# A four-layer hybrid backbone: one activation on ScalarE and two steps on VectorE take another place in the order

## The chip, the cores and the metric

The kernel runs on one core of a Trainium2 chip. The core has five engines that run their own instruction streams and meet at semaphores: TensorE (PE, matrix products), VectorE (DVE), ScalarE (ACT), GpSimd (POOL) and SyncE (SP), which here only issues loads. The time of a run is the device time of one execution in microseconds. Of the kernel before there are three runs.

## The reference

Four layers run over 256 context tokens and 256 latent tokens of width 1024, with the mixers A, B, C, A. A is a bidirectional Mamba-2 (SSD) mixer, B grouped-query attention, C a pooling mixer. Each layer is modulated by a vector (shift, scale, gate) from a matrix product with `mod_w`, and ends in a layer norm:

```python
for i in range(DEPTH):
    shift_x, scale_x, gate_x = split(sc @ mod_w[i] + mod_b[i], 3)
    hx = x * (1 + scale_x) + shift_x                  # the same for hc from ctx
    out_x, out_c = mixer(hx, hc, ...)                 # A, B, C, A
    x = layer_norm(ALPHA * x + gate_x * out_x)        # and ctx, but for the last layer
```

The pooling mixer (layer 2) splits its projection into `u` and `z`. `u` falls into four groups of 512 channels, each with a window of 2, 4, 8 or 16 tokens:

```python
pooled = centred_mean(u_g, window) - u_g
out = ((pooled @ group_w[g]) * layer_scale * silu(z_g)) @ w_out
```

The SSD mixer (layers 0 and 3) projects to x, B, C and a gate z, passes x, B and C through a depthwise convolution of 5 taps and a SiLU, and scans forwards and backwards in chunks of 128 tokens. Within a chunk the scores C B^T are masked (lower triangle forwards, upper backwards), weighted by head and by decay, and applied to x. In the last layer only the latent tokens' output is wanted, so only the two latent chunks are scored.

## The kernel before

All products with weights are made from fp32 values split in two: ACT copies a loaded unit to a rounded high half (`act_split`, L377), DVE subtracts it for the low half (`dve_split`, L384), and PE makes three passes (`three_pass`, L415 to L417). A unit is 128 x 1024 values, 512 KB. SP loads the units in the order of the list `items` into `raw`, a ring of four slots. A slot is loaded again once the unit in it is used up: for a weight, once its low half is written (`lo_done`), for a piece of `mod_w`, once PE has summed it (`mod_summed`). The weights themselves sit in a ring of four pairs.

The order of the work is written out by hand, for each engine on its own; there is no scheduler. Each engine runs its stream in order.

Layer 3 (SSD) goes over eight groups in a pipeline: step i projects group i and scans group i - 1. PE projects tiles 0 to 3 (two of x, one of B, one of C) and two of z into PSUM banks. On ACT, `ssd_act_step` makes the middle tap of tile k (`first_tap(k)`, L735), and on DVE `ssd_dve_step` adds the other four (`taps(k)`, L901). DVE's `masks()` (L919) makes the forward and the backward masked scores `cb` of the scanned group; `cb_dt(n)` on ACT (L766) weights the backward ones of chunk n, four heads each, and `weigh_steps` on DVE (L928) adds the forward part that POOL made. The order on DVE in a step is `taps(0)`, `masks()`, `gate` (L980), `taps(1)`, then the two splits of z, `weigh_steps`, and so on. Layer 0 has the same functions; it runs `first_tap(1)` behind `cb_dt`, where layer 3 runs it in front.

Layer 2 (pooling) goes over four groups g. PE projects four tiles of u, then four of z, and after each of the first three z tiles it sums one piece of the next layer's modulation (`pe_mod_sum`, L444), and turns the one before it (`pe_mod_turn`, L469) after ACT has copied its rows (L464). Then it applies the group weights. For each u tile t, ACT copies it to `up`; DVE makes the window sums (`lev`, L2348, one instruction for a window of 2 up to four for 16), scales (L2358) and subtracts (L2360) into `pf`; ACT rounds `pf` to `p_hi` (L2329) and DVE subtracts for `p_lo` (L2366). In between, DVE splits the four units of z: two, called (g, 0), after tile 1's sums, two, called (g, 1), in front of tile 3's. The list `items` has for each group: four units of u, four of z, six of modulation (three pieces of two halves), two of group weights. So the six modulation units follow the z units through the ring: the first piece takes the slots of z (g, 0), the second those of z (g, 1), the third those of the first. DVE also adds the bias to each turned piece (`dve_mod_col`, L476) and in groups 0 and 1 scales and shifts the residual (`dve_resid`, L1549 and L1553, four instructions over 1024 columns).

Of the kernel before, what the change touches and what calls it, by code (L numbers as in the profile page):

```python
# [3 lines left out]
def backbone(nc, ins, out, depth=4):  # L4
# [153 lines left out]
    def last_layer(L):  # L158
        return L == DEEP - 1
# [44 lines left out]
    for L in range(depth):  # L204
        more = L + 1 < depth
# [173 lines left out]
    def dve_split(dve, *key, width=UNIT):  # L379
        r = R_OF[key]  # L380
        hi, lo = w_place(key)
        dve.wait_ge(raw_full[r % RS], LOADS[r])
        dve.wait_ge(hi_done, W_OF[key] + 1)
        dve.tensor_tensor(lo[:, 0:width], raw[:, r % RS, 0:width], hi[:, 0:width].bitcast(F32),  # L384
                          ALU.subtract).then_inc(lo_done, 1)
# [20 lines left out]
    def dve_split2(dve, *key):  # L406
        for a in range(2):
            dve_split(dve, *key, a)
# [22 lines left out]
    def mod_at(L, q):  # L431
        return MOD_PIECES * L + q
# [40 lines left out]
    def dve_mod_col(dve, L, q, b, col=0):  # L473
        dve.wait_ge(mod_turned, mod_at(L, q) + 1)
        bias = par[:, 0, 24 * L + 2 * q:24 * L + 2 * q + 2].unsqueeze(2).broadcast_to((128, 2, 2))
        dve.tensor_tensor(mod_col[:, L % 2, 2 * q:2 * q + 2, :],  # L476
                          bank[b][:, col:col + 4].rearrange("p (t s) -> p t s", s=2), bias,
                          ALU.add).then_inc(mod_done, 1)
# [7 lines left out]
    def p_poolscale():  # L486
        return par[:, 1, 64:80]
# [17 lines left out]
    def scan_done(L, g, name):  # L505
        jobs = scan_jobs(L)
        return len(jobs) * g + jobs.index(name) + 1
# [7 lines left out]
    def proj_bank(i, k):  # L515
        return bank[proj_index(i, k) % 4]
# [15 lines left out]
    def c_of(g):  # L532
        return xcc[:, :] if g % 2 else xc[:, 3, :]
# [182 lines left out]
    def ssd_act_step(act, L, i):  # L716
        s = lay[L]
        g = i - 1
# [5 lines left out]
        def first_tap(k):  # L724
            if k == 3:
                if i >= 2:
                    act.wait_ge(s["scan_p"], scan_done(L, i - 2, "it3"))
                dst, a = c_of(i), t0
            else:
                if g >= 0:  # L730
                    act.wait_ge(s["t1_p"], 4 * g + (4 if k == 2 else k + 1))
                dst, a = xc[:, k, :], 0
            what = "x" if k < 2 else "bc"
            act.wait_ge(s[what + "_p"], 3 * i + 1 + 2 * (k % 2))
            act.activation(dst[:, a:], proj_bank(i, k)[:, a:], ACT.Identity, scale=gp[:, i, 6 * k + 2:6 * k + 3],  # L735
                           bias=gp[:, i, 6 * k + 5:6 * k + 6]).then_inc(s["tap_a"], 1)
# [23 lines left out]
        def cb_dt(n):  # L760
            c = first + n
            act.wait_ge(s["cbm_d"], 2 * g + 2)
            if nc * g + n >= 2:
                act.wait_ge(s["m_d"], nc * g + n - 1)
            for h in range(HG):
                last = act.activation(Wb[:, n % 2, h, :], cb[:, 1, c, :], ACT.Copy,  # L766
                                      scale=sg[:, g, 48 + 4 * c + h:49 + 4 * c + h])
            last.then_inc(s["cbdt_a"], 1)
# [63 lines left out]
        if has_ssd:  # L832
            turned()
        first_tap(0)
        if last_layer(L):
            first_tap(1)
        if has_ssd:
            cb_dt(0)
            cb_dt(1)
        if not last_layer(L):  # L840
            first_tap(1)
        if i == 0:
            first_tap(2)
            ssd_act_cum(act, L)
# [551 lines left out]
    def dve_ylo(dve, L, c):  # L1396
        s = lay[L]
        t0 = SEG if last_layer(L) else 0
        dve.wait_ge(s["yhi_a"], c + 1)
        hi = yhi_of(L, c)[:, t0:].bitcast(F32)  # L1400
        if L % 3 == 0:
            dve.wait_ge(s["sq_a"], c + 1)
            dve.scalar_tensor_tensor(ylo[:, c, t0:], ys[:, c, t0:], p_normg(L // 3)[:, c:c + 1], hi,
                                     ALU.mult, ALU.subtract).then_inc(s["ylo_d"], 1)
        else:
            dve.tensor_tensor(ylo[:, c, t0:], ys[:, c, t0:], hi, ALU.subtract).then_inc(s["ylo_d"], 1)
# [136 lines left out]
    def dve_resid(dve, L, tiles):  # L1543
        s = lay[L]
        dve.wait_ge(s["ln_loaded"], s["base"]["ln_loaded"] + 32)
        for n, tt in enumerate(out_tiles(L + 1)):
            if tt in tiles:
                dve.wait_ge(s["turn_p"], s["base"]["turn_p"] + 2 * tt + 2)
                dve.tensor_tensor(resid[:, tt, :], resid[:, tt, :], lng_b[:, :], ALU.mult).then_inc(s["resid_d"], 1)  # L1549
        dve.wait_ge(s["resid_d"], s["base"]["resid_d"] + resid_count(L, tiles, 1))  # L1550
        for n, tt in enumerate(out_tiles(L + 1)):
            if tt in tiles:
                dve.tensor_tensor(resid[:, tt, :], resid[:, tt, :], lnb_b[:, :], ALU.add).then_inc(s["resid_d"], 1)  # L1553
# [666 lines left out]
    def pool_steps(w):  # L2220
        return [m for m in (2, 4, 8, 16) if m <= w]
# [4 lines left out]
    def pool_tile_end(n):  # L2226
        g, t = divmod(n, 4)
        return pool_ops_before(g) + (t + 1) * (len(pool_steps(WINDOWS[g])) + 2)
# [102 lines left out]
    def pool_dve(dve, L):  # L2331
        s = lay[L]
        more = L + 1 < depth
        T = Tally(s["pool_d"])
        for g in range(4):
            w = WINDOWS[g]
            for t in range(4):
                n = 4 * g + t
                dve.wait_ge(s["up_a"], n + 1)
                if t == 3:  # L2340
                    dve_split2(dve, L, "z", (g, 1))
                src = up[:, t % 2, :, :]
                for lv, m in enumerate(pool_steps(w)):
                    a, b = PADL - w // 2, PADL - w // 2 + SEG + w - m
                    dst = lev[:, lv % 2, :, :]
                    if T.n:
                        T.wait(dve)
                    T.inc(dve.tensor_tensor(dst[:, :, a:b], src[:, :, a:b], src[:, :, a + m // 2:b + m // 2], ALU.add))  # L2348
                    src = dst
                T.wait(dve)  # L2350
                if n:
                    dve.wait_ge(s["plo_d"], n)
                    dve.wait_ge(s["phi_a"], n)
                else:
                    dve.wait_ge(s["tab_loaded"], 16)
                a = PADL - w // 2
                inv = invc[:, g, :].unsqueeze(1).broadcast_to((128, 2, SEG))
                T.inc(dve.tensor_tensor(two(pf[:, :]), src[:, :, a:a + SEG], inv, ALU.mult))  # L2358
                T.wait(dve)
                T.inc(dve.tensor_tensor(two(pf[:, :]), two(pf[:, :]), up[:, t % 2, :, PADL:PADL + SEG], ALU.subtract))  # L2360
                assert T.n == pool_tile_end(n)
                if t == 1:
                    dve_split2(dve, L, "z", (g, 0))
                dve.wait_ge(s["phi_a"], n + 1)
                T.wait(dve)
                dve.tensor_tensor(p_lo[:, t, :], pf[:, :], p_hi[:, t, :].bitcast(F32), ALU.subtract).then_inc(s["plo_d"], 1)  # L2366
            if more:
                dve_mod_col(dve, L + 1, 3 * g, 6)
            if g < 2:
                dve_resid(dve, L - 1, (2 * g, 2 * g + 1))  # L2370
            if more:
                dve_mod_col(dve, L + 1, 3 * g + 1, 7)
            dve_split2(dve, L, "gw", g)
            if more:
                dve_mod_col(dve, L + 1, 3 * g + 2, 6)
            if g == 3:
                for c in range(4):
                    dve_ylo(dve, L, c)
            for t in range(4):
                n = 4 * g + t  # L2380
                dve.wait_ge(s["mix_p"], 5 * g + t + 1 + t // 3)
                dve.wait_ge(s["zs_a"], 4 * g + 4)
                dve.scalar_tensor_tensor(ys[:, n, :], bank[6 + t % 2], p_poolscale()[:, n:n + 1], zs[:, t, :],
                                         ALU.mult, ALU.mult).then_inc(s["mix_d"], 1)
                if g < 3 and t == 1:
                    dve_split2(dve, L, "u", (g + 1, 0))
                if g == 3 and t == 1:
                    for c in range(2):
                        dve_split(dve, L, "out", c, 0)
            if g < 3:  # L2390
                dve_split2(dve, L, "u", (g + 1, 1))
        for c in (2, 3):
            dve_split(dve, L, "out", c, 0)
        for c in range(4, 12):
            dve_ylo(dve, L, c)
        for c in range(4, 12):
            dve_split(dve, L, "out", c, 0)
        dve_out(dve, L, 12)
# [237 lines left out]
```

## Time and profile before

| | |
|---|---|
| median of 3 runs | 1572.9 us (1571.96 to 1574.02) |
| the profiled execution | 1572.9 us, span 1571.7 us |
| PE busy | 1469.3 us (93% of the span) |
| DVE busy | 1129.2 us (72%) |
| ACT busy | 712.8 us (45%) |
| POOL busy | 328.8 us (21%) |
| granted TensorE clock, mean | 0.970 |
| layer 2, group 1 of the pooling, of 60.00 us | PE busy 59.59, DVE 32.99, ACT 17.68 us |

The busy shares are means over four layers with different limits, and overlapping matmuls count as busy. What a place is worth is seen from its own stretch. In a timeline row the columns are the start in us from the span's start, the length in us, the engine, the line in the kernel, the operation, out<-in with the tiles' names (`ps` is PSUM) and shapes, and xN where N instructions were merged; in brackets is the idle time before it and what ended it. Rows of one engine may overlap a little, since an instruction begins before the one in front has quite ended.

### The profile page before, as it was taken

The numbers are of one execution on the slowest core, as the hardware profiler recorded it, in microseconds if no ns is written. First come the engines' busy times: TensorE is split into PE (matmuls) and PEld (weight loads), VectorE is DVE, ScalarE is ACT, GpSimd is POOL, SyncE is SP. The second block draws the span as 40 slices with busy tenths as digits, with TensorE's granted clock in tenths as the row PEclk, the third lists the DMA queues.
The fourth block names the chain that finished last, engine by engine and source line by source line (L and its number), as shares of the span: only waits on it lengthen the run. The fifth ranks groups of instructions, "written<-read, shape, count | busy, mean of one in ns | idle before, by whom it ended". The sixth has DMA issues, their size and how long they took to land.

```text
span 1571.7 us, 22693 instructions
## 1 busy us (share of the span) xinstructions
PE 1469.3 (93%) x8557; PEld 1215.8 (77%) x8557; DVE 1129.2 (72%) x1680; ACT 712.8 (45%) x1271; POOL 328.8 (21%) x379
## 2 busy tenths in 40 slices
PE   5889999999998998997989999999998899999987
PEld 3768888888877898775658877877787788888865
DVE  0688999999984467555557645645436899999986
ACT  1554554454552253355454423223424556565552
POOL 1043344434441010001000000000000144443440
PEclk7999999999999999899999999999999999999998
DMA  9245644556443311314332245354241343443433
GB/s 322 73 133 161 175 120 135 161 161 187 136 133 105 124 44 54 121 30 149 118 122 94 85 158 188 101 167 153 82 134 40 88 134 108 123 119 108 121 130 126
DMA packets 169420, 197.38 MB, mean 126 GB/s; under 512 B 9696, under 2 KB 151648, under 8 KB 169312
## 3 DMA queue, kind: packets, MB, share of 16 engines
q1 hardware_dynamic: 158480, 163.08, 32.9%
q0 software_dynamic: 9296, 30.19, 7.4%
q10 hardware_dynamic: 1536, 2.67, 0.5%
q8 instruction: 68, 1.11, 0.3%
q14 instruction: 40, 0.33, 0.1%
HBM read 194.59 MB, written 1.31 MB: 125 GB/s over the span
## 4 chain that ended last, share of the span: by engine, by line
PE 49%; DVE 33%; issue 8%; ACT 7%; SPq 2%; DMA 1%; POOL 1%; DVEq 0%; ACTq 0%
PE ps L415 13%; PE ps L416 12%; PE ps L417 12%; DVE xc L901 7%; DVE w_lo L384 5%; DVE cum_b L909 3%; ACT w_hi L377 2%; ACT Wb L766 2%; PE ps L444 2%; SPq L2413 1%; DVE Wb L928 1%; PE ps L596 1%; PE ps L1862 1%; DVE Hs L946 1%; PE ps L602 1%
## 5 line engine op out<-in xcount | busy, mean ns | idle before, releaser
L415 PE MATMUL ps<-h_hi,w_hi 128*128 128x512 f32 (+2 forms) x1088 | 413.0, 380 | 10.3 <-DVE w_lo L384 5.4
L416 PE MATMUL ps<-h_lo,w_hi 128*128 128x512 f32 (+2 forms) x1088 | 399.6, 367 | 0.0
L417 PE MATMUL ps<-h_hi,w_lo 128*128 128x512 f32 (+2 forms) x1088 | 399.4, 367 | 0.0
L384 DVE TENSOR_TENSOR w_lo<-raw,w_hi 128x1024 fp32r<-128x1024 f32 (+1 forms) x205 | 246.5, 1236 | 142.9 <-ACT w_hi L377 141.3
L377 ACT ACTIVATE w_hi<-raw 128x1024 fp32r<-128x1024 f32 (+1 forms) x205 | 208.4, 1049 | 130.1 <-PE ps L417 113.0
L415 PEld LDWEIGHTS ps<-h_hi,w_hi 128*128 128x128 f32 (+1 forms) x1088 | 206.3, 190 | 60.3 <-issue 26.0
L417 PEld LDWEIGHTS ps<-h_hi,w_lo 128*128 128x128 f32 (+1 forms) x1088 | 206.1, 189 | 33.8
L416 PEld LDWEIGHTS ps<-h_lo,w_hi 128*128 128x128 f32 (+1 forms) x1088 | 206.5, 190 | 30.6
L901 DVE SCALAR_TENSOR_TENSOR xc<-ps,gp,xc 128x508 f32<-128x508 f32 (+1 forms) x224 | 162.7, 728 | 19.4 <-ACT xc L735 13.4
L417 PE MATMUL ps<-w_hi,ylo 128*128 128x512 f32 x384 | 150.4, 392 | 0.0
L1105 POOL DMA_DIRECT2D cum_b<-cum_scratch x96 | 71.8, 754 | 249.1 <-PE ps L596 168.0
L415 PE MATMUL ps<-w_hi,h_hi 128*128 128x512 f32 (+1 forms) x336 | 120.1, 357 | 2.4 <-DVE ys L980 1.0
L416 PE MATMUL ps<-w_lo,h_hi 128*128 128x512 f32 (+1 forms) x336 | 117.3, 349 | 0.0
L1750 POOL TENSOR_TENSOR small<-small 128x1 f32<-128x1 f32 x14 | 10.4, 740 | 469.9 <-DVE small L1685 469.9
L1124 POOL TENSOR_TENSOR xw<-xT,sg 128x256 f32<-128x256 f32 x96 | 80.1, 865 | 84.8 <-ACT xT L757 84.8
L417 PEld LDWEIGHTS ps<-w_hi,ylo 128*128 128x128 f32 x384 | 72.6, 189 | 15.5
L766 ACT ACTIVATE Wb<-cb,sg 128x128 f32<-128x128 f32 x192 | 58.8, 390 | 46.4 <-DVE cb L919 46.4
L415 PEld LDWEIGHTS ps<-w_hi,h_hi 128*128 128x128 f32 x336 | 65.3, 194 | 15.4 <-issue 6.0
L476 DVE TENSOR_TENSOR mod_col<-ps,par 128x4 f32<-128x4 f32 x48 | 7.6, 159 | 93.0 <-PE ps L469 93.0
L909 DVE TENSOR_TENSOR cum_b<-cum_b,sg 128x1024 f32<-128x1024 f32 x48 | 73.4, 1529 | 0.1
L1134 POOL TENSOR_TENSOR Wa<-cb,sg 128x512 f32<-128x512 f32 x48 | 58.9, 1247 | 57.8 <-DVE Wb L928 37.6
L416 PEld LDWEIGHTS ps<-w_lo,h_hi 128*128 128x128 f32 x336 | 65.2, 194 | 7.3
(258 smaller groups left out, 2617.1 us busy)
## 6 DMA issues: line engine op xcount, KB each, us to landing
raw<-in_mod_w SPq DMA_DIRECT2D x80, 512.0 KB, 4.6
raw<-in_ssm_w_in SPq DMA_DIRECT2D x64, 512.0 KB, 4.8
cum_b<-cum_scratch POOLq DMA_DIRECT2D x96, 256.0 KB, 5.7
raw<-in_ssm_w_in SPq DMA_DIRECT2D x66, 256.0 KB, 4.4
raw<-in_ssm_w_out SPq DMA_DIRECT2D x32, 512.0 KB, 4.7
raw<-in_pool_w_in SPq DMA_DIRECT2D x32, 512.0 KB, 4.8
raw<-in_attn_w_in SPq DMA_DIRECT2D x20, 512.0 KB, 3.9
raw<-in_pool_w_out SPq DMA_DIRECT2D x16, 512.0 KB, 4.3
```

The costliest lines, as they stand in the source:

```text
L377: act.activation(w_place(key)[0][:, 0:width], raw[:, r % RS, 0:width], ACT.Copy).then_inc(hi_done, 1)
L384: dve.tensor_tensor(lo[:, 0:width], raw[:, r % RS, 0:width], hi[:, 0:width].bitcast(F32), ALU.subtract).then_inc(lo_done, 1)
L415: pe.matmul(o, hi_s, hi_m, start=first, stop=False)
L416: pe.matmul(o, hi_s, lo_m, start=False, stop=False)
L417: return pe.matmul(o, lo_s, hi_m, start=False, stop=last)
L444: last = pe.matmul(bank[b][32 * j:32 * j + 32, 0:256], c_col[:, 4 * a + j, :], w[:, 256 * j:256 * j + 256], start=a == 0, stop=a == 1)
L766: last = act.activation(Wb[:, n % 2, h, :], cb[:, 1, c, :], ACT.Copy, scale=sg[:, g, 48 + 4 * c + h:49 + 4 * c + h])
L901: T["tap_d"].inc(dve.scalar_tensor_tensor(ov, iv, gp[:, i, 6 * k + tap:6 * k + tap + 1], ov, ALU.mult, ALU.add))
L909: T["seg_d"].inc(dve.tensor_tensor(e, e, by_head(sg[:, g, 8 * c:8 * c + 8], (128, 8, 128)), ALU.subtract))
L1105: pool.dma_start(cum_b[:, c, d, :, :], src).then_inc(s["cum_loaded"][c], 16)
L1124: last = pool.tensor_tensor(xw[:, k, d, :].rearrange("p (h q) -> p h q", q=PH), xT[:, cs[d], :].rearrange("p (h q) -> p h q", q=PH), sprea ...
L1134: pool.tensor_tensor(Wa[:, n % 2, :, :], cb[:, 0, c, :].unsqueeze(1).broadcast_to((128, HG, 128)), spread(sg[:, g, 32 + 4 * c:36 + 4 * c], ...
```

## The change

Three places change. In layer 3, ACT makes the first tap of tile 1 after the two `cb_dt`, as in layer 0. In layer 2, DVE splits z (g, 1) after tile 3's sums, in the place after tile 3 that (g, 0) has after tile 1. And in layer 2 the first of the three `dve_mod_col` of a group comes after `dve_resid`.

```diff
         first_tap(0)
-        if last_layer(L):
-            first_tap(1)
         if has_ssd:
             cb_dt(0)
             cb_dt(1)
-        if not last_layer(L):
-            first_tap(1)
+        first_tap(1)
...
                 dve.wait_ge(s["up_a"], n + 1)
-                if t == 3:
-                    dve_split2(dve, L, "z", (g, 1))
                 src = up[:, t % 2, :, :]
...
-                if t == 1:
-                    dve_split2(dve, L, "z", (g, 0))
+                if t % 2:
+                    dve_split2(dve, L, "z", (g, t // 2))
                 dve.wait_ge(s["phi_a"], n + 1)
                 T.wait(dve)
                 dve.tensor_tensor(p_lo[:, t, :], pf[:, :], p_hi[:, t, :].bitcast(F32), ALU.subtract).then_inc(s["plo_d"], 1)
-            if more:
-                dve_mod_col(dve, L + 1, 3 * g, 6)
             if g < 2:
                 dve_resid(dve, L - 1, (2 * g, 2 * g + 1))
             if more:
+                dve_mod_col(dve, L + 1, 3 * g, 6)
                 dve_mod_col(dve, L + 1, 3 * g + 1, 7)
```

ACT in step 1 of layer 3, before, from the high halves of B and C to the next tap:

```order
485 L377 ACTIVATE w_hi<-raw 128x1024 x2
486 L757 ACTIVATE xT<-ps 128x4x128 x2
487 L757 ACTIVATE BT<-ps 128x512
488 L735 ACTIVATE xc<-ps,gp 128x512 x2
489 L766 ACTIVATE Wb<-cb,sg 128x128 x8
490 L741 ACTIVATE xc<-xc 128x512
491 L377 ACTIVATE w_hi<-raw 128x1024 x2
```

The same place after the change:

```order
485 L377 ACTIVATE w_hi<-raw 128x1024 x2
486 L757 ACTIVATE xT<-ps 128x4x128 x2
487 L757 ACTIVATE BT<-ps 128x512
488 L735 ACTIVATE xc<-ps,gp 128x512
489 L766 ACTIVATE Wb<-cb,sg 128x128 x8
490 L735 ACTIVATE xc<-ps,gp 128x512
491 L741 ACTIVATE xc<-xc 128x512
492 L377 ACTIVATE w_hi<-raw 128x1024 x2
```

One of the two taps (L735) now stands behind the eight weightings (L766), in front of the SiLU (L741). The same happens in each of the steps 1 to 7.

DVE in group 3 of layer 2, before, from `p_lo` of tile 2 to `p_lo` of tile 3 and the modulation columns:

```order
907 L2366 TENSOR_TENSOR p_lo<-pf,p_hi 128x512
908 L384 TENSOR_TENSOR w_lo<-raw,w_hi 128x1024 x2
909 L2348 TENSOR_TENSOR lev<-up 128x2x270
910 L2348 TENSOR_TENSOR lev<-lev 128x2x268
911 L2348 TENSOR_TENSOR lev<-lev 128x2x264
912 L2348 TENSOR_TENSOR lev<-lev 128x2x256
913 L2358 TENSOR_TENSOR pf<-lev,invc 128x512
914 L2360 TENSOR_TENSOR pf<-pf,up 128x512
915 L2366 TENSOR_TENSOR p_lo<-pf,p_hi 128x512
916 L476 TENSOR_TENSOR mod_col<-ps,par 128x4 x2
```

The same place after the change, where the lines have moved up by 5:

```order
905 L2361 TENSOR_TENSOR p_lo<-pf,p_hi 128x512
906 L2343 TENSOR_TENSOR lev<-up 128x2x270
907 L2343 TENSOR_TENSOR lev<-lev 128x2x268
908 L2343 TENSOR_TENSOR lev<-lev 128x2x264
909 L2343 TENSOR_TENSOR lev<-lev 128x2x256
910 L2353 TENSOR_TENSOR pf<-lev,invc 128x512
911 L2355 TENSOR_TENSOR pf<-pf,up 128x512
912 L384 TENSOR_TENSOR w_lo<-raw,w_hi 128x1024 x2
913 L2361 TENSOR_TENSOR p_lo<-pf,p_hi 128x512
914 L476 TENSOR_TENSOR mod_col<-ps,par 128x4 x2
```

The two splits (L384) have moved behind the six instructions of the sums. In groups 0, 1 and 2 there are three, four and five such instructions.

DVE in group 1 of layer 2 at the residual, before:

```order
842 L2366 TENSOR_TENSOR p_lo<-pf,p_hi 128x512
843 L476 TENSOR_TENSOR mod_col<-ps,par 128x4
844 L1549 TENSOR_TENSOR resid<-resid,lng_b 128x1024 x2
845 L1553 TENSOR_TENSOR resid<-resid,lnb_b 128x1024 x2
846 L476 TENSOR_TENSOR mod_col<-ps,par 128x4
```

The same place after the change:

```order
841 L2361 TENSOR_TENSOR p_lo<-pf,p_hi 128x512
842 L1546 TENSOR_TENSOR resid<-resid,lng_b 128x1024 x2
843 L1550 TENSOR_TENSOR resid<-resid,lnb_b 128x1024 x2
844 L476 TENSOR_TENSOR mod_col<-ps,par 128x4 x2
845 L384 TENSOR_TENSOR w_lo<-raw,w_hi 128x1024 x2
```

The first column now stands next to the second, behind the residual.

## Rows read from the trace of the kernel before

**Rows 1.** Stretches: length, busy us (instructions) per engine, clock, DMA share, GB/s; a step

```profile
core 0: us, PE busy (x) PEld busy (x) DVE busy (x) ACT busy (x) POOL busy (x), PEclk, DMA share, GB/s
1288.05:1322.73 34.68, 33.88 (x202) 29.84 (x201) 33.48 (x44) 19.49 (x34) 14.92 (x16) 1.00 0.44 125
```

**Rows 2.** Waits, 1253 to 1500 us, of DVE and of PE: total, times, longest

```profile
DVE w_lo L384 <- ACT w_hi L377: 6.0, 9, 1.8
...
PE ps L415 <- DVE w_lo L384: 2.9, 7, 0.5
```

**Rows 3.** Timeline of ACT, layer 3, step 2

```profile
1294.84 0.78 ACT L735 ACTIVATE xc<-ps,gp 128x512 f32<-128x512 f32 x1 [4.63 <-PE ps L417]
1297.11 2.46 ACT L766 ACTIVATE Wb<-cb,sg 128x128 f32<-128x128 f32 x8 [1.49 <-DVE cb L919]
1299.47 0.62 ACT L741 ACTIVATE xc<-xc 128x512 f32<-128x512 f32 x1
```

**Rows 4.** Timeline of DVE, layer 3, step 2

```profile
1293.33 3.08 DVE L901 SCALAR_TENSOR_TENSOR xc<-ps,gp,xc 128x508 f32<-128x508 f32 x4
1296.33 0.42 DVE L919 TENSOR_TENSOR cb<-ps,upto 128x256 f32<-128x256 f32 x1
...
1297.65 3.09 DVE L901 SCALAR_TENSOR_TENSOR xc<-ps,gp,xc 128x508 f32<-128x508 f32 x4
1301.14 2.36 DVE L384 TENSOR_TENSOR w_lo<-raw,w_hi 128x1024 fp32r<-128x1024 f32 x2 [0.40 <-ACT w_hi L377]
```

**Rows 5.** Timeline of ACT, layer 0: tile 1's first tap behind `cb_dt`

```profile
300.13 0.76 ACT L735 ACTIVATE xc<-ps,gp 128x512 f32<-128x512 f32 x1
```

**Rows 6.** Timeline of DVE, layer 0: tile 1's four taps

```profile
300.92 3.10 DVE L901 SCALAR_TENSOR_TENSOR xc<-ps,gp,xc 128x508 f32<-128x508 f32 x4 [0.77 <-ACT xc L735]
```

**Rows 7.** Timeline of DVE, layer 2, group 3

```profile
1077.76 2.35 DVE L384 TENSOR_TENSOR w_lo<-raw,w_hi 128x1024 fp32r<-128x1024 f32 x2
1080.03 0.72 DVE L2348 TENSOR_TENSOR lev<-up 128x540 f32<-128x540 f32 x1
...
1083.73 0.69 DVE L2360 TENSOR_TENSOR pf<-pf,up 128x512 f32<-128x512 f32 x1
```

**Rows 8.** Timeline of SP: the second modulation piece's second half, groups 0 to 3

```profile
899.27 0.37 SPq L2425 DMA_DIRECT2D raw<-in_mod_w  x1
...
958.32 0.37 SPq L2425 DMA_DIRECT2D raw<-in_mod_w  x1
...
1018.68 0.37 SPq L2425 DMA_DIRECT2D raw<-in_mod_w  x1
...
1080.14 0.37 SPq L2425 DMA_DIRECT2D raw<-in_mod_w  x1
```

**Rows 9.** Landing: second half in group 3, in group 1; first half

```profile
raw<-in_mod_w SPq DMA_DIRECT2D x1, 512.0 KB, 5.5
...
raw<-in_mod_w SPq DMA_DIRECT2D x1, 512.0 KB, 5.1
...
raw<-in_mod_w SPq DMA_DIRECT2D x1, 512.0 KB, 3.6
```

**Rows 10.** Timeline of PE: the second modulation piece, groups 0 to 3

```profile
904.74 1.07 PE L444 MATMUL ps<-raw,c_col 128*32 128x256 f32 x16
...
964.66 1.07 PE L444 MATMUL ps<-raw,c_col 128*32 128x256 f32 x16
...
1024.58 1.07 PE L444 MATMUL ps<-raw,c_col 128*32 128x256 f32 x16
...
1085.89 0.61 PE L469 MATMUL ps<-pick,mod_rows 128*128 128x2 f32 x4 [1.68 <-ACT mod_rows L464]
1086.43 1.07 PE L444 MATMUL ps<-raw,c_col 128*32 128x256 f32 x16
```

**Rows 11.** DVE by shape, the step of rows 1: count, busy us, mean ns

```profile
L911 DVE TENSOR_TENSOR cum_b<-cum_b 128x512 f32<-128x512 f32 x2 | 2.1, 1047 | 0.1
L928 DVE TENSOR_TENSOR Wb<-Wb,Wa 128x512 f32<-128x512 f32 x2 | 1.8, 957 | 0.0
...
L934 DVE TENSOR_TENSOR cum_b<-cum_b,Wb 128x512 f32<-128x512 f32 x2 | 1.3, 684 | 0.0
```

## The prediction

> **What bounds the kernel now.** I read the busy share and clock by stretch first, then who waited for whom, then the timelines of ScalarE (ACT) and VectorE (DVE) around the moved lines, and last the queue and the landings of the loads. The change touches two of the four layers, and they have different limits. The last layer is an SSD layer whose groups repeat every 34.68 us. In one such step DVE is busy 33.48 us and TensorE (PE) 33.88 us, at a granted clock of 1.00 [rows 1]. Both look full, so the waits decide. In the seven steps and what follows them DVE waited 6.0 us in all, always for ScalarE's high half of a weight; PE waited for DVE's low half seven times, 2.9 us in all [rows 2]. The reader is to see that DVE never waits for PE: its own program, in order, sets the pace and has 0.4 us of slack in a step. In the pooling layer it is the reverse: PE works nearly without a break, and DVE has long waits. There DVE's work is free until it holds up something that PE needs, and that can be a buffer of a transfer.
>
> **Part 1, last layer: the first tap of the second x tile goes behind the backward mask weights.** No instruction is added. Before, ACT did this tap at 1294.84, once PE had filled the bank, then idled 1.49 us until DVE's masks came, and did eight mask weightings from 1297.11; its next instruction began at 1299.47, 2.36 us on [rows 3]. DVE did four taps of tile 0 (3.00 us from start to next start), masks, gate, and began the four taps of tile 1 at 1297.65 with no wait [rows 4]. Now ACT begins the weightings at the same time, since they wait for the masks and not for ACT, and the tap only at 1299.47. How long DVE then waits is shown by layer 0, which already has this order: ACT's tap began at 300.13 and DVE's at 300.92, 0.79 us later, with DVE waiting [rows 5, 6]. So DVE's taps of tile 1 start at 1299.47 + 0.79 = 1300.26, 2.61 us late, and end 3.00 us later, at 1303.26. The next instruction on DVE is the split of z, which before began at 1301.14 after a 0.40 us wait for ACT [rows 4]. ACT's split moves by one tap (0.78) only and is ready by then, so that wait disappears: 1303.26 - 1301.14 = 2.12 us of DVE lost in a step.
>
> Nothing takes this back within a step. DVE's 33.48 busy plus 2.61 of wait is over 34.68, and the wait closes a loop (DVE masks, ACT weightings, ACT tap, DVE taps) that PE is not in. Queued behind DVE's wait are the z split, for which PE already waits 0.4 us, and then the states. ACT's later work (second SiLU, squares, exponentials) hangs on DVE's taps and moves with it by less than 2.12. The order has the new sequence in seven steps (groups 1 to 7). 7 x 2.12 = 14.8 us. Bounds: at least 0 if PE's schedule had room to swallow all, at most 7 x 2.61 = 18.3 if the 0.40 is not won back.
>
> **Part 2, pooling layer: the split of the second z pair goes behind the pooling of tile 3.** Per group DVE now does the window sums of tile 3 first (3, 4, 5, 6 instructions in groups 0 to 3), then the two splits. In group 3 the splits began at 1077.76 and the sums at 1080.03; the last of the six began at 1083.73 [rows 7], a pitch of 0.74, and I estimate that it hands over 0.61 after its start, since its row gives 0.69 and the pair of splits hands over 0.08 before its end (1083.73 + 0.61 = 1084.34). The sums thus last 1084.34 - 1080.03 = 4.31 us, and the splits move by that in group 3 and by one pitch less for each level less: 3.57, 2.83, 2.09 in groups 2, 1, 0. PE itself needs these weights for z tile 2, which follows the sum begun at 1086.43 [rows 10]; they are ready at 1077.76 + 4.31 + 2.35 = 1084.4, so directly it costs nothing.
>
> But the split also frees the staging slots. The ring has four slots, and the two halves of this z pair hold those into which SyncE (SP) loads the second modulation piece, one slot for each half. SP waits in order for exactly these splits: the load of the second half was issued at 1080.14, as the split ended; in the other groups at 899.27, 958.32 and 1018.68 [rows 8]. It landed 5.5 us later in groups 0 and 3 and 5.1 in group 1 (I take 5.5 for group 2); the first half, issued 1.1 us before with no company, took 3.6 [rows 9]. PE sums this piece in two halves of 0.5 us right after z tile 1: sums started at 904.74, 964.66, 1024.58 and 1086.43 [rows 10], so the second half was read at 905.24, 965.16, 1025.08, 1086.93. Before, the piece was there in time each time, by 0.5 to 1.7 us. Now:
> group 0: 899.27 + 2.09 + 5.5 = 906.86, PE waits 1.6;
> group 1: 958.32 + 2.83 + 5.1 = 966.25, PE waits 1.1;
> group 2: 1018.68 + 3.57 + 5.5 = 1027.75, PE waits 2.7;
> group 3: 1080.14 + 4.31 + 5.5 = 1089.95, later than before by 3.0.
> In group 3 PE had waited 1.68 us for ACT's modulation rows [rows 10], since ACT was held by tile 3's high half, whose sums now come 2.3 us sooner. That wait vanishes, but what is late next is this load, and the 3.0 is already counted from the old time. Sum 8.4 us. PE has nearly no other wait in this layer to absorb them, and all that follows starts later. Bounds: the gain of 1.7 alone if the loads come in time; 16 if each landing took 2 us more than taken.
>
> The Trainium skill, "DMA: Bandwidth & Descriptors", section on the anatomy of one DMA, gives about 2.0 us fixed plus bytes over 436 GB/s, as an estimate 3.2 us for these 512 KB. By it only groups 2 and 3 would wait, some 1.1 us, and the whole would be about 1589. The lone half's 3.6 is near it and the second half's 5.5 is not, so the trace does not agree for loads that share the engines, and I keep 5.5.
>
> **Part 3: the modulation column is added after the residual's scaling.** In groups 0 and 1 four 1024-wide instructions (about 4.7 us, by the 2.35 for two in [rows 7]) now go ahead of it. Before, DVE sat idle there until PE had turned the column. PE wants it only before its sum after z tile 2, one projection on. In group 1 the scaling also releases POOL's load of the next norm rows some 3 us sooner, beside the group weights' load, which has a margin of several us. Cost 0; if that margin were gone, up to 1 us.
>
> **The sum.** The profiled execution took 1572.9 us with a span of 1571.7, and the median of the runs is the same 1572.9. 14.8 + 8.4 = 23.2, so 1596.1.
>
> **Rivals.**
> A, the forecast: both costs stand, 1590 to 1602. Chance 0.60.
> B, the loads are hidden after all: the later loads have less company and land in the 3.6 us of [rows 9]. Then groups 0 and 1 don't wait, group 2 waits 0.8 and group 3 is 1.1 later than before: 14.8 + 1.9, 1589.6. For it: the first half does so. Against: the first modulation piece's slots are free by then, so SP issues the third piece's loads right behind the second half as before. Chance 0.12.
> C, relief on DVE: some of its instructions in a step are stretched while POOL works. The pairs of minima and of weight sums took a mean of 1047 and 957 ns where the same shape elsewhere took 684 [rows 11]. With DVE moved 2.12 us against POOL they could shrink: 2 x 0.363 + 2 x 0.273 = 1.27 us in a step. The first of the seven has no squares on POOL to be free of, so 6 x 1.27 = 7.6 less, 1588.5. Against: POOL's squares wait for ACT, which waits for DVE's taps, so they move by about 1.5 us too. Chance 0.13.
> The Trainium skill, "GPSIMD Engine Reference", section Specifications, says that GpSimd shares its SBUF interface with VectorE's instructions that have two SBUF inputs. The stretched ones are of that kind, so the trace agrees; the rule gives this rival's mechanism and not its size.
> D, not slower: PE's rate and not DVE's sets both layers, so DVE's lateness is swallowed and only ACT's 1.68 us wait goes: 1571.2. Its place is ACT's tap in the last layer, which waited 4.63 us for PE [rows 3]; it decides once DVE's busy time and wait fit into a step. For it: PE is busy 33.88 of 34.68. Against: 33.48 + 2.61 = 36.1 does not fit. Chance 0.05.
> E, more than forecast: the second half lands as late as the loads behind it, about 2 us more, in four groups: 1604. Chance 0.10.
>
> **The numbers.** The time is that of A, 1596.1. The range takes in B and C and stops short of E's end: 1586 to 1603. A difference under 0.2% (3.1 us) can't be told from no change. A, B, C and E are all slower than that, 0.95; D is split, 0.03 same and 0.02 faster.
>
> **What would show it.** In the last layer DVE's taps of xc should show seven waits of about 2.6 us for ACT's L735, and the step should be 36.8 us long. PE's wait for the low halves should grow by 2 us a step. In the pooling layer PE's sums (L444) should wait for a DMA in all four groups, 8 us in all, and the wait for ACT's modulation rows should be gone. A step that stays near 34.7 us breaks part 1; four groups without a DMA wait break part 2; a clock under 1.00 in either layer would add a cost that I don't count.

## The result and the profile after

The changed kernel takes 1601.4 us (median of 4 runs, 1596.3 to 1607.0) against 1573.5 us (4 runs, 1572.0 to 1574.1): ratio 1.0177, 95% interval 1.0151 to 1.0203, or 28.0 us slower. The forecast was 1596.1 with a range of 1586 to 1603. The profiled execution took 1598.8 us, with a span of 1597.6, 25.9 us over that of before.

In the last layer step 2, counted from one first set of taps to the next, in the busy shares by stretch (columns as in [rows 1]):

```profile
1306.61:1343.12 36.51, 33.89 (x196) 29.84 (x195) 33.17 (x44) 19.47 (x33) 12.98 (x16) 0.95 0.41 117
```

DVE's busy time is 33.17 us, 0.3 less than in [rows 1], and the step is 36.51 us long instead of 34.68. The waits of DVE and then of PE from 1265 to 1520 us say where the rest is:

```profile
DVE xc L898 <- ACT xc L735: 17.9, 8, 3.2
...
PE ps L596 <- DVE Hs L948: 11.1, 6, 2.6
PE ps L415 <- DVE w_lo L384: 1.6, 4, 0.5
```

DVE, which never waited for a tap in [rows 2], now waits 17.9 us for ACT's. PE's new wait is not for the low halves of z as I had written but a little further on, for the states (L948); before, the same wait was short (PE's waits, 1253 to 1500 us):

```profile
PE ps L596 <- DVE Hs L951: 2.2, 6, 0.4
```

The timeline of ACT in this step, against [rows 3]:

```profile
1310.39 2.46 ACT L766 ACTIVATE Wb<-cb,sg 128x128 f32<-128x128 f32 x8 [6.92 <-DVE cb L916]
1312.75 0.77 ACT L735 ACTIVATE xc<-ps,gp 128x512 f32<-128x512 f32 x1
```

and of DVE, against [rows 4]:

```profile
1306.61 3.08 DVE L898 SCALAR_TENSOR_TENSOR xc<-ps,gp,xc 128x508 f32<-128x508 f32 x4
...
1313.55 3.10 DVE L898 SCALAR_TENSOR_TENSOR xc<-ps,gp,xc 128x508 f32<-128x508 f32 x4 [2.54 <-ACT xc L735]
1316.56 2.35 DVE L384 TENSOR_TENSOR w_lo<-raw,w_hi 128x1024 fp32r<-128x1024 f32 x2
```

The idle time of ACT in front of the weightings has grown from 1.49 to 6.92 us, since the tap that stood in the middle of it is behind them now. DVE's taps start 0.80 us after ACT's tap (1313.55 against 1312.75), as in layer 0 [rows 5, 6].

The seven steps are not all alike. DVE's masks of the first scanned group and those that follow the seventh step bound them, before and then after:

```profile
1262.61 0.42 DVE L919 TENSOR_TENSOR cb<-ps,upto 128x256 f32<-128x256 f32 x1
...
1505.16 0.41 DVE L919 TENSOR_TENSOR cb<-ps,upto 128x256 f32<-128x256 f32 x1
```

```profile
1273.76 0.41 DVE L916 TENSOR_TENSOR cb<-ps,upto 128x256 f32<-128x256 f32 x1
...
1530.46 0.41 DVE L916 TENSOR_TENSOR cb<-ps,upto 128x256 f32<-128x256 f32 x1
```

They took 242.55 us and take 256.70, 14.15 more: from mask row to mask row the steps grew by 2.13, 1.84, 2.24, 1.77, 2.25, 1.82 and 2.10 us.

In the pooling layer, PE at the second modulation piece, groups 0 and 3, against [rows 10]:

```profile
903.74 0.64 PE L444 MATMUL ps<-raw,c_col 128*32 128x256 f32 x8
905.83 0.64 PE L444 MATMUL ps<-raw,c_col 128*32 128x256 f32 x8 [1.45 <-DMA raw<-in_mod_w]
906.40 0.59 PE L415 MATMUL ps<-h_hi,w_hi 128*128 128x512 f32 x1
906.79 0.63 PE L416 MATMUL ps<-h_lo,w_hi 128*128 128x512 f32 x1
...
910.15 0.39 PE L415 MATMUL ps<-h_hi,w_hi 128*128 128x512 f32 x1
...
1092.34 0.50 PE L469 MATMUL ps<-pick,mod_rows 128*128 128x2 f32 x4
1095.31 0.64 PE L444 MATMUL ps<-raw,c_col 128*32 128x256 f32 x8 [2.48 <-DMA raw<-in_mod_w]
1097.91 1.08 PE L444 MATMUL ps<-raw,c_col 128*32 128x256 f32 x8 [1.96 <-DMA raw<-in_mod_w]
```

The sum was one row without a wait; now PE waits for the load, in groups 2 and 3 for both halves. In group 1 it waits 1.31 us, in group 2 0.33 and 2.33. In group 3 the load of the second half was issued at 1092.72 (timeline of SP, against [rows 8]) and took 5.2 us (landings, against [rows 9]):

```profile
1092.72 0.37 SPq L2419 DMA_DIRECT2D raw<-in_mod_w  x1
```

```profile
raw<-in_mod_w SPq DMA_DIRECT2D x1, 512.0 KB, 5.2
```

What I had not priced stands in the rows at 906.40 and 906.79: behind the wait the matmuls take 0.59 and 0.63 us instead of 0.39, until about 910. The busy shares by stretch show why (the clock is the third number from the right):

```profile
905.00:911.00 6.00, 5.17 (x21) 3.83 (x22) 0.82 (x2) 0.38 (x1) 0.00 (x0) 0.72 0.90 320
963.00:973.00 10.00, 8.69 (x53) 6.54 (x52) 5.66 (x7) 0.98 (x2) 1.05 (x2) 1.00 0.97 300
1031.00:1037.00 6.00, 5.29 (x22) 3.88 (x23) 0.00 (x0) 0.39 (x1) 0.00 (x0) 0.72 0.85 302
1098.00:1103.00 5.00, 5.00 (x21) 3.40 (x22) 0.00 (x0) 0.38 (x1) 0.00 (x0) 0.68 0.92 331
```

The granted clock is a mean of its two levels, 2.4 GHz (1.00) and 1.2 GHz (0.50). Behind the waits of groups 0, 2 and 3 it fell; behind the 1.31 us of group 1 it did not. Before the change it was 1.00 through the whole layer, also behind PE's stand of 1.68 us [rows 10].

The layer's whole cost can be read from two rows of DVE on each side: the subtraction of group 0's first tile, which marks the start, and the first output product of group 3. Of before and then of after:

```profile
884.07 0.69 DVE L2360 TENSOR_TENSOR pf<-pf,up 128x512 f32<-128x512 f32 x1
...
1104.01 0.75 DVE L2383 SCALAR_TENSOR_TENSOR ys<-ps,par,zs 128x512 f32<-128x512 f32 x1
```

```profile
883.25 0.69 DVE L2355 TENSOR_TENSOR pf<-pf,up 128x512 f32<-128x512 f32 x1
...
1116.58 0.75 DVE L2377 SCALAR_TENSOR_TENSOR ys<-ps,par,zs 128x512 f32<-128x512 f32 x1
```

From 219.94 us it has grown to 233.33, so 13.4 us. The waits for the load are 1.45 + 1.31 + 2.66 + 4.44 = 9.86; less the 1.68 that went, 8.2. Of the other 5.2 us, 4.7 are the slow matmuls when their starts are set against those behind group 1's wait (1.6, 1.6 and 1.5 us in groups 0, 2 and 3); the last 0.5 is not assigned.

The account of the 25.9 us then is: 13.4 in the pooling layer, 14.15 in the seven steps, less 0.8 (the pooling layer began 0.8 us earlier) and less 1.4 at the start of the last layer, which leaves 0.5 for the end. The 1.4 us are not traced to the change: PE stood 3.5 us there in both kernels, and behind it the mean granted clock over 6 us was 0.50 before (1212 to 1218 us) and 0.75 after (1224.5 to 1230.5). DVE's wait for PE that follows is 2.8 us before and 1.4 after, and between 1.6 and 2.8 in the traces of the experiments.

### The profile page after: what moved, and what is told of

It is laid out like the page before. It is cut to its first block and busy times, and to the rows that moved or that the text cites. A ratio compares the mean times of both kernels' runs of the same rounds, so it can differ in the third digit from the quotient of the medians.

```text
span 1597.6 us, 22697 instructions
## 1 busy us (share of the span) xinstructions
PE 1481.6 (93%) x8557; PEld 1224.2 (77%) x8557; DVE 1126.8 (71%) x1680; ACT 713.3 (45%) x1271; POOL 322.2 (20%) x379
## 3 DMA queue, kind: packets, MB, share of 16 engines
q10 hardware_dynamic: 1536, 2.67, 0.5%
HBM read 194.59 MB, written 1.31 MB: 123 GB/s over the span
## 5 line engine op out<-in xcount | busy, mean ns | idle before, releaser
L384 DVE TENSOR_TENSOR w_lo<-raw,w_hi 128x1024 fp32r<-128x1024 f32 (+1 forms) x205 | 245.2, 1229 | 139.8 <-ACT w_hi L377 138.1
L1121 POOL TENSOR_TENSOR xw<-xT,sg 128x256 f32<-128x256 f32 x96 | 76.6, 830 | 88.7 <-ACT xT L757 88.7
L766 ACT ACTIVATE Wb<-cb,sg 128x128 f32<-128x128 f32 x192 | 58.8, 389 | 77.5 <-DVE cb L916 77.5
L906 DVE TENSOR_TENSOR cum_b<-cum_b,sg 128x1024 f32<-128x1024 f32 x48 | 76.1, 1585 | 0.1
```

Of the source, the lines that this page charges most:

```text
L906: T["seg_d"].inc(dve.tensor_tensor(e, e, by_head(sg[:, g, 8 * c:8 * c + 8], (128, 8, 128)), ALU.subtract))
L1121: last = pool.tensor_tensor(xw[:, k, d, :].rearrange("p (h q) -> p h q", q=PH), xT[:, cs[d], :].rearrange("p (h q) -> p h q", q=PH), sprea ...
```

## The experiments

Each was timed beside the kernel before; the ratio goes by those runs.

**The first edit alone.** The hunk of `first_tap` in the diff above, on the kernel before.

> Only the first of the three edits: in the last layer ScalarE makes tile 1's first tap behind the two sets of mask weights. Theory (the wait of VectorE for this tap costs each of the seven steps about 1.85 us, as the trace after shows, and is independent of the pooling layer): about 13 us over the kernel before, 1586, with seven waits of 2.5 us or more for ScalarE's tap. Rival (the last layer only reshuffles what the pooling layer's delay already cost, or PE's own rate swallows it): within 4 us of the kernel before.

Measured: 1588.1 us, ratio 1.0091 (1.0077 to 1.0105), 14.3 us. The trace has DVE's waits for the tap, 18.0 us in all from 1200 to 1520 us, and its seven steps take 256.69 us, as in the changed kernel (256.70). The theory holds and the rival falls. The 13 us expected were too few because they took the growth of one step, 1.85, for all seven; the mean is 2.02.

**The second edit alone.** The hunk that moves the splits of z (g, 1).

> Only the second edit: VectorE splits the second z pair behind the sums of tile 3 in the pooling layer. Theory (late release of two staging slots, late load, PE waits 8.2 us net, and after three of the waits TensorE runs some us at its lower clock): about 13 us over the kernel before, 1586, with PE waiting for the modulation piece in all four groups and slower matmuls behind some waits; its times should scatter by several us, as those of the changed kernel do, if the falls of the clock come and go. Rival (load only, the clock's fall is of the last layer's making): 8 us, 1581, and little scatter.

Measured: 1585.6 us, ratio 1.0076 (1.0063 to 1.0090), 12.0 us. PE waits 9.6 us for the modulation pieces, and the clock falls behind two of the waits (stretches as above):

```profile
PE ps L444 <- DMA raw<-in_mod_w: 9.6, 5, 2.4
```

```profile
908.00:914.00 6.00, 5.40 (x22) 4.00 (x23) 3.44 (x3) 0.39 (x1) 0.00 (x0) 0.72 0.88 310
1095.00:1105.00 10.00, 6.69 (x30) 4.40 (x31) 0.00 (x0) 0.38 (x1) 0.00 (x0) 0.66 0.82 278
```

The cost is as expected. PE's stand in group 2 was 2.29 us here, about what it was in the changed kernel (2.33), and the clock did not fall behind it:

```profile
1034.15 0.64 PE L444 MATMUL ps<-raw,c_col 128*32 128x256 f32 x8 [2.29 <-DMA raw<-in_mod_w]
```

```profile
1034.00:1040.00 6.00, 5.85 (x31) 4.56 (x32) 0.00 (x0) 0.38 (x1) 0.00 (x0) 1.00 0.77 277
```

So whether a stand is followed by a fall differs from execution to execution. The wide scatter that was expected did not come (1584.8 to 1587.2), but five runs are few for it.

**The third edit alone.** `dve_mod_col` behind `dve_resid`.

> Only the third edit: the first modulation column is added behind the residual's scaling. Theory: nothing waits for it, 0 us, within 1 us of the kernel before. Rival (the earlier load of the norm rows gets in the way of the others): 1 to 2 us slower.

Measured: 1575.5 us, ratio 1.0008 (0.9995 to 1.0021): not to be told from no change. PE's waits in the layer are the same five as before. But in this trace the clock fell behind one of them, PE's stand of 1.66 us for ACT's rows in group 3 (stretch as above), and the layer is 1.6 us longer by the two rows of DVE used above; in the kernel before the same stand, 1.68 us, has no fall behind it.

```profile
1087.34 0.61 PE L469 MATMUL ps<-pick,mod_rows 128*128 128x2 f32 x4 [1.66 <-ACT mod_rows L464]
```

```profile
1090.00:1095.00 5.00, 5.00 (x18) 3.96 (x18) 0.00 (x0) 0.00 (x0) 0.00 (x0) 0.74 0.56 203
```

The 1.3 us thus need no cause in the third edit.

**The late split without the slots.** The second edit, and in the list of loads:

```diff
                 for t in range(2):
                     add_piece("w", L, "z", (g, t))
-                for q in range(3):
-                    add_piece("m", L + 1, "mod", 3 * g + q) if more else None
+                    add_piece("m", L + 1, "mod", 3 * g + t) if more else None
+                add_piece("m", L + 1, "mod", 3 * g + 2) if more else None
```

> The second edit, and in the pooling layer another order of the loads: the two first modulation pieces go in front of and behind the second z pair, so that the second piece takes the slots of the first piece and no longer those that the late split frees. VectorE's order is that of the second edit. Theory (only the slots make the late split dear): the 13 us vanish, 1570 to 1575, with no wait of PE for the second piece, no slow matmuls behind it and a scatter like that of the kernel before. Rival (VectorE's lateness costs by itself, through the weights or the sums): 1580 or more.

Measured: 1571.8 us, ratio 0.9988 (0.9976 to 1.0000). In PE's waits of the layer no wait for a load is left, the one for ACT's rows is 0.7 instead of 1.68, and the sum of group 3 is one row again:

```profile
PE ps L469 <- ACT mod_rows L464: 0.7, 1, 0.7
```

```profile
1086.44 1.07 PE L444 MATMUL ps<-raw,c_col 128*32 128x256 f32 x16
```

DVE splits as late as in the changed kernel, and it costs nothing. The 12 us were the slots'. The new order of loads was not run with DVE's old order; what it could hide there is small, since PE's only wait that it shortens is that for ACT's rows, by 1.0 us.

**Keeping PE at work while it waits.** The second edit, and in `pe_mod_sum` of the second piece:

```diff
         for a in range(2):
+            for _ in range(fill[a]):
+                pe.matmul(bank[0][:, 0:256], h_hi[:, 0, 0:128], h_hi[:, 0, 256:512], start=True, stop=True)
```

with `fill` (0, 10), (0, 9), (2, 18), (20, 14) for groups 0 to 3 (how many of these idle matmuls, whose results nobody reads, stand ahead of each half of the piece), behind a wait for ACT's copy out of that bank, long past.

> The second edit alone, and in PE's waits for the second modulation piece some 10 to 34 matmuls of 256 columns (0.12 us each) into a bank that nobody reads, ahead of and between its two halves; their results are not used. Theory (PE's stand while it waits makes the granted clock fall, and that costs up to 5 us of the edit's 12): the waits for the load shrink by what the matmuls take and the load still lands as late, but no matmul of 0.63 us follows and the granted clock stays at 1.00 through the pooling layer; 1579 to 1583, 2 to 5 us under the kernel with this edit alone. Rival (the fall comes from something else, such as the load's own traffic): the clock falls as before and the time is the same 1585.6 or more.

Measured: 1581.3 us, ratio 1.0040 (1.0024 to 1.0055), 6.3 us: 5.7 less than with the second edit alone, each of the two known to about 2 us. Timeline of PE, group 3, and the stretches around the waits of groups 0 and 3:

```profile
1090.22 2.64 PE L437 MATMUL ps<-h_hi 128*128 128x256 f32 x20
1092.88 0.64 PE L446 MATMUL ps<-raw,c_col 128*32 128x256 f32 x8
1093.44 1.93 PE L437 MATMUL ps<-h_hi 128*128 128x256 f32 x14
1095.42 0.64 PE L446 MATMUL ps<-raw,c_col 128*32 128x256 f32 x8
```

```profile
903.00:914.00 11.00, 11.00 (x77) 8.55 (x80) 4.96 (x6) 1.84 (x4) 0.00 (x0) 1.00 0.76 251
1090.00:1104.00 14.00, 13.94 (x103) 11.00 (x102) 1.66 (x5) 3.23 (x5) 0.00 (x0) 1.00 0.70 231
```

The load lands as late as without the idle matmuls (5.2 us in group 0, 5.1 in group 3), and the clock stays at 1.00 in the whole layer. By the two rows of DVE used above, the layer is 12.4 us longer than before with the second edit alone and 8.3 with the idle matmuls: the 8.3 are what the late loads cost, and the other 4.1 the slower clock, of two falls in that trace. That the fall comes from PE's standing, and that it is worth 4 to 6 us of the 12, is shown. Only one execution of this kernel was profiled, and falls do come and go, but here four stands in a row were filled and none has a fall behind it.

**Work in DVE's wait.** The first edit, and `decay(1)` in the last layer in front of `taps(1)` instead of behind `weigh_steps(1)`.

```diff
+        if has_ssd and last_layer(L):
+            decay(1)
         taps(1)
...
             weigh_steps(1)
-            decay(1)
+            if not last_layer(L):
+                decay(1)
```

> The first edit, and on VectorE in the last layer the decay of the second chunk (1.95 us in two instructions) in front of the taps of tile 1 instead of behind the weight sums. Theory (the 14 us of the first edit are VectorE standing still): the wait of 2.54 becomes about 0.6 in each step, which is what the vanished 0.40 wait for the high half was, so the loss falls from 14 to 0 to 3 us, 1573 to 1577. Rival (VectorE's place in the step is what matters, z's low halves for PE come late all the same): PE waits for them and the time stays over 1583.

Measured: 1573.4 us, ratio 0.9988 (0.9975 to 1.0000). Timeline of DVE:

```profile
1289.73 2.79 DVE L384 TENSOR_TENSOR w_lo<-raw,w_hi 128x1024 fp32r<-128x1024 f32 x2
...
1299.34 1.29 DVE L906 TENSOR_TENSOR cum_b<-cum_b,sg 128x1024 f32<-128x1024 f32 x1
1300.67 1.42 DVE L908 TENSOR_TENSOR cum_b<-cum_b 128x512 f32<-128x512 f32 x1
1302.01 3.09 DVE L898 SCALAR_TENSOR_TENSOR xc<-ps,gp,xc 128x508 f32<-128x508 f32 x4
...
1324.30 2.78 DVE L384 TENSOR_TENSOR w_lo<-raw,w_hi 128x1024 fp32r<-128x1024 f32 x2
```

The wait is gone altogether: the two instructions take 2.67 us there instead of the 1.95 that I had expected. The step is 34.57 us, 0.11 shorter than before, and the whole loss of the first edit is back. The earlier decay was not run without the first edit; DVE's wait that it could take away there is the 0.40 us of [rows 4] a step, far from 14.3 us in seven steps.

**Half the distance.** The first tap of tile 1 between `cb_dt(0)` and `cb_dt(1)`.

> The tap of tile 1 between the two sets of mask weights, one chunk's four weightings (1.2 us) in front of it instead of eight. Theory (the loss is the wait less the 0.40 that it replaces): the wait of 2.54 becomes about 1.35, the loss about 0.7 to 0.95 us a step, 5 to 7 us in all, 1579 to 1581. Rival (a threshold: any tap behind the masks misses the step): 12 us or more, 1586.

Measured: 1580.6 us, ratio 1.0040 (1.0026 to 1.0054), 6.3 us. DVE's taps of tile 1 in this kernel:

```profile
1300.59 3.10 DVE L902 SCALAR_TENSOR_TENSOR xc<-ps,gp,xc 128x508 f32<-128x508 f32 x4 [1.36 <-ACT xc L735]
```

With half the weightings in front, about half of the 2.54 us of wait and 6.3 of the 14.3 us are left. No threshold shows between the two places.

**All three edits with both mends.**

> All three edits kept, with the two mends: the order of loads of the fourth experiment, and the decay of the sixth in VectorE's wait. Theory (the slots and VectorE's wait are the two causes and there is no third): 1570 to 1576, at or near the kernel before. Rival (the edits have a cost together that neither has alone, such as the clock): 1580 or more.

Measured: 1571.9 us, ratio 0.9986 (0.9974 to 0.9997). With the slots and DVE's wait mended no loss is left. At 0.14% under the kernel before it is no more than such a measurement can tell from no change.

## Why the prediction was right, and where it was short

Direction, mechanisms and the forecast's own case (A) were right, and 1601.4 lies within its 1590 to 1602 and the range. That it does is in part luck: the sum was 5.3 us short, and the width that covers this was there for other things. The three edits apart cost 14.3, 12.0 and 1.3 us, together 27.6 of the 28.0, each known to about 2 us.

Part 1, last layer. The predicted wait of 2.61 us was 2.54, and seven steps at 2.12, 14.8 us, measured 14.3 alone and 14.15 in the trace. Three of the steps grew by 1.8 only. In one of these, and the step of [rows 1], read by shape, the minima (L908 after the change) had a mean of 839 ns where [rows 11] has 1047, twice a step, and the subtractions of decays (L906) one of 1694 where it was 1421, twice too, so some shrank and some grew. That they met POOL's instructions at other moments fits this but no run shows it. Over the seven steps DVE's busy time fell from 231.79 to 230.50 us: rival C was there with 1.3 us in all, not 7.6. The first of the seven waits was longer, 3.19 us, as that step has no gate in between. Which of its results PE then waits for I had wrong: not the low halves of z but the states that DVE makes later in the step. The price came out the same; that it must, since both hang on the same lateness, is argued and not shown.

Part 2, pooling layer. The waits for the load were forecast as 1.6, 1.1, 2.7 and 3.0 us, 8.4 in all; they were 1.45, 1.31, 2.66 and 4.44 - 1.68 = 2.76, together 8.2. The landing times of before, 5.1 to 5.5 us, were the right ones to take (5.2 in group 3), and with them rival B fell; so did E. The experiment with other slots shows that the slots of the ring, and nothing else in DVE's lateness, made these waits.

The step that failed is the sum's silence on the clock. The text named it among the signs ("would add a cost that I don't count") and put 0 for it, without a reason. It was about 5 us in the changed kernel's trace (4.7 read off the matmuls, 5.2 as what the waits leave), and the experiment that kept PE at work puts it at 4.1 us by the traces and 5.7 by the times. With 5.2 the second edit's 8.4 becomes 13.6, and the sum 28.4, against 28.0. That it closes so well is again in part luck: the changed kernel's trace has other terms that no part of the sum had, such as the 1.4 us regained at the start of the last layer, and the second edit alone measured 12.0. No row of the pooling layer before could warn of the term, for its clock is 1.00 throughout; but the mean clock of 0.970 is short of 1.00 somewhere, the stretch from 1212 to 1218 us shows 0.50 behind a stand of PE, and I looked only at a stretch that had 1.00.

Part 3 was put at 0: 1.3 us with an interval that holds 0, and the trace has a fall of the clock for it. D, that DVE's lateness is swallowed, fell by the first experiment; it needed 36.1 us of DVE to fit into 34.68.

The changed kernel's times lie over 10 us (1596.3 to 1607.0), where each edit alone has some 3 us in four and five runs. That it scatters more is not shown: the kernel before, which lay within 2.1 us in its first four runs, lies between 1568.8 and 1579.3 in the 28 runs timed beside the later experiments.

## What to carry to other kernels

When an instruction is put later on an engine with slack, look first at what its end releases: here two staging slots of a ring, and through them a load that had 0.5 to 1.7 us to spare. On an engine without slack, a wait that closes a loop with another engine was paid nearly in full here (2.0 us a step for a wait of 2.5 that replaced one of 0.4), and came back when independent work was put into it. And price a new wait of TensorE with the slower clock that may follow it: here it added 4 to 5 us to 8 us of waits.

## What the runs showed of the hardware

A short stand of TensorE can be dear. Behind a stand of 1.45 us between two sets of narrow matmuls (32 columns of weights) nine matmuls took 0.6 instead of 0.39 us, at a mean granted clock of 0.72 over 6 us; behind a like stand of 1.31 us it stayed at 1.00. The length of the stand does not settle it: behind 2.33 us the clock fell in the changed kernel and behind 2.29 us at the same place it did not with the second edit alone; behind 1.66 us it fell with the third edit alone and behind 1.68 us at the same place it did not in the kernel before. With idle matmuls in the stands it stayed at 1.00 in the whole layer. In the last layer the clock fell too (0.95 over the step shown), with DVE setting the pace there, and the step, 36.51 us, is DVE's busy 33.17, its wait of 2.54 and 0.80 of small gaps, the same 0.80 that the step before has (34.68 less 33.48 and 0.40). So the fall cost nothing there.

Two loads of 512 KB from one queue that are issued 1.1 us apart do not land alike: the first took 3.6 to 3.8 us in all four groups after the change and the second 5.2 to 5.7, against 3.5 to 3.6 and 5.1 to 5.5 before. The Trainium skill, "DMA: Bandwidth & Descriptors", section on the anatomy of one DMA, has 2.0 us plus the bytes over 436 GB/s for a transfer issued from GpSimd, an estimated 3.2 us for 512 KB. These loads are issued from SyncE, which the prediction did not say when it used the figure; the first load comes near it all the same and the second, with more behind it in the queue, does not.
